# Inverting the heads' triangular matrices on 32x32 diagonal blocks, all four at once, with two slots for the modulation tiles

## What is computed

```python
decay = jnp.exp(jnp.where(lower, g[..., :, None] - g[..., None, :], -jnp.inf))
L = jnp.where(strict, jnp.einsum('bhncd,bhnsd->bhncs', kb, k) * decay, 0.0)
T = lax.linalg.triangular_solve(eye + L, jnp.broadcast_to(eye, L.shape),
                                left_side=True, lower=True, unit_diagonal=True)
u = T @ vb
w = T @ (kb * jnp.exp(g)[..., None])
# then, chunk by chunk: v_new = u - w S;  o = q_dec S + attn v_new;  S = S * g_last + k_dec^T v_new
```

## Time and profile before

| | |
|---|---|
| three executions | 1651.15, 1651.70, 1654.02 us |
| the profiled execution | 1650.68 us, its span 1649.0 us |
| mean granted TensorE clock in the span | 0.997 |
| busy: PE, DVE, ACT, POOL | 97%, 68%, 58%, 30% |
| the rounds, from the first L2410 to the first L2515 | 198.4 to 361.3 us of the span |
| one round | 20.7 us |

### The profile page before, as it was taken

How to read it: one execution, slowest core, us unless ns; L and a number is a source line. 1 busy time by engine, 2 the same in 40 slices (tenths; PEclk the granted TensorE clock), 3 DMA queues, 4 the chain that set the end, 5 groups by cost and what they waited for, 6 DMA issues and landing times.

```text
span 1649.0 us, 33605 instructions
## 1 busy us (share of the span) xinstructions
PE 1594.5 (97%) x11469; PEld 1482.8 (90%) x11477; DVE 1126.0 (68%) x2361; ACT 949.8 (58%) x1811; POOL 491.9 (30%) x406
## 2 busy tenths in 40 slices
PE   7999999999999999999999999999999999999998
PEld 6899899999898899889999999899999888888886
DVE  3787767755556574586469889889898555555554
ACT  1765566664465554563444444689898555544454
POOL 3000256647000005000037777766666100000000
PEclk9999999999999999999999999999999999999999
DMA  9668211138353245247535555554444556666553
GB/s 292 219 185 279 78 52 52 53 121 257 108 154 103 93 158 179 77 128 184 123 112 169 170 173 166 161 152 141 137 138 132 178 191 192 193 193 196 192 191 128
DMA packets 211818, 255.67 MB, mean 155 GB/s; under 512 B 15911, under 2 KB 193803, under 8 KB 211723
## 3 DMA queue, kind: packets, MB, share of 16 engines
q1 hardware_dynamic: 211723, 254.39, 50.5%
HBM read 253.29 MB, written 1.05 MB: 154 GB/s over the span
## 4 chain that ended last, share of the span: by engine, by line
PE 65%; issue 19%; POOL 9%; DVE 3%; ACT 2%; DMA 2%; SPq 1%; POOLq 0%; another core or an unknown queue 0%; DVEq 0%; ACTq 0%
PE ps L2825 21%; PE ps L2234 14%; PE ps L2807 9%; POOL w_lo L721 8%; PE ps L2795 3%; PE ps L2426 2%; PE ps L2515 2%; PE ps L2410 2%; PE ps L2254 1%; PE ps L2406 1%; DMA arena<-in_ada_w 1%; PE ps L2592 1%; POOL arena L711 0%; PE ps L2612 0%; PE ps L2329 0%
## 5 line engine op out<-in xcount | busy, mean ns | idle before, releaser
L721 POOL TENSOR_TENSOR w_lo<-raw,w_hi 128x1024 fp32r<-128x1024 f32 x128 | 307.6, 2407 | 331.7 <-ACT w_hi L1247 331.4
L2234 PE MATMUL ps<-x_hi,w_hi 128*128 128x256 f32 x1088 | 315.2, 290 | 8.1 <-DVE w_lo L1378 3.0
L2234 PE MATMUL ps<-x_lo,w_hi 128*128 128x256 f32 x1088 | 308.3, 283 | 0.0
L2234 PE MATMUL ps<-x_hi,w_lo 128*128 128x256 f32 x1088 | 308.2, 283 | 0.0
L2193 DVE TENSOR_TENSOR w_lo<-raw,w_hi 128x1024 fp32r<-128x1024 f32 x124 | 152.0, 1225 | 143.3 <-ACT w_hi L1356 143.3
L1356 ACT ACTIVATE w_hi<-raw 128x1024 fp32r<-128x1024 f32 x124 | 131.6, 1061 | 167.9 <-PE ps L2825 167.9
L2234 PEld LDWEIGHTS ps<-x_hi,w_hi 128*128 128x128 f32 x1088 | 209.0, 192 | 14.5 <-issue 5.8
L2234 PEld LDWEIGHTS ps<-x_lo,w_hi 128*128 128x128 f32 x1088 | 209.2, 192 | 1.3 <-issue 1.2
L2234 PEld LDWEIGHTS ps<-x_hi,w_lo 128*128 128x128 f32 x1088 | 209.0, 192 | 0.0
L1247 ACT ACTIVATE w_hi<-raw 128x1024 fp32r<-128x1024 f32 x128 | 134.9, 1054 | 110.3 <-DVE raw L1995 110.2
L2770 PE MATMUL ps<-x_hi,w_hi 128*128 128x256 f32 x576 | 165.1, 287 | 9.5 <-ACT arena L1269 8.2
(11 more groups left out here) (432 smaller groups left out, 3734.9 us busy)
## 6 DMA issues: line engine op xcount, KB each, us to landing
raw<-in_u_experts SPq DMA_DIRECT2D x512, 128.0 KB, 2.6
raw<-in_v_experts SPq DMA_DIRECT2D x128, 512.0 KB, 4.3
arena<-in_ada_w SPq DMA_DIRECT2D x22, 1024.0 KB, 7.8
raw<-in_a_w_in SPq DMA_DIRECT2D x12, 1024.0 KB, 5.8
arena<-in_a_w_in SPq DMA_DIRECT2D x12, 1024.0 KB, 5.5
raw<-in_b_w_in SPq DMA_DIRECT2D x8, 1024.0 KB, 5.5
arena<-in_b_w_in SPq DMA_DIRECT2D x8, 1024.0 KB, 5.5
raw<-in_w_in SPq DMA_DIRECT2D x8, 1024.0 KB, 5.4
```

The lines of the kernel that those rows point to most:

```text
L721: pool.tensor_tensor(UTL[e], UT[e % 2], UTH[e].bitcast(F32), ALU.subtract).then_inc(utl_ready, 1)
L2234: ins = mm(o[:, b * S:b * S + S], w[:, slot, kk, b * P:b * P + P], xx[:, (kk + turn) % KC, :], start=(kk == 0 and n == 0), stop=(kk == k - ...
```

## The change

Levels 0 to 3, up to blocks of 32, now touch only the sixteen 32x32 diagonal blocks of the four matrices, packed in one 128x128 tile XC (block q of matrix m in partitions q to q+31 and columns 32m to 32m+31). Each product is 32 deep and 32 wide; the second of a level has 16 moving columns. The transposed copy XC_T is made by DVE (`v.transpose`, within 32x32 blocks) in place of PE's transposition and ACT's copy. Level 4 works on 32x32, level 5 on 64x64 blocks; their results go straight to INVT, the transposed inverse that `finish` reads, and ACT spreads the diagonal blocks into it (`spread`). g no longer alternates.

```diff
+            def diagonal_blocks():
+                return [(m, q, m // 2, 128 * (m % 2) + q) for m in range(4) for q in (0, 32, 64, 96)]
+            def setup_low(r):
+                pe.wait_ge(h_lt, r.nth(1))
+                for m, q, g, at_ in diagonal_blocks():
+                    ins = mm(LOWC[q:q + 32, 32 * m:32 * m + 32], LT[r.side][g][q:q + 32, at_:at_ + 32], ident[q:q + 32, q:q + 32],
+                             start=True, stop=True)
+                ins.then_inc(h_xT, 1)
             def level_p(r, j):
...
-                        for cc in range(2):
-                            ins = pe.transpose(B_[g][:, 256 + cc * 128:384 + cc * 128], xx[:, cc * 128:cc * 128 + 128], ident)
...
+                if j < 4:
+                    for m, q, g, at_ in diagonal_blocks():
+                        ins = mm(PA[q:q + 32, 32 * m:32 * m + 32], lt[g][q:q + 32, at_:at_ + 32], XC[q:q + 32, m, :],
+                                 start=True, stop=True)
+                elif j == 4:
+                    for m, q, g, at_ in diagonal_blocks():
+                        if q % 64 == 0:
+                            ins = mm(PA[q + 32:q + 64, 32 * m:32 * m + 32], lt[g][q:q + 32, at_ + 32:at_ + 64], XC[q:q + 32, m, :],
+                                     start=True, stop=True)
...
+                ins.then_inc(h_p, 1)
             def level_d(r, j):
...
+                if j < 4:
+                    for m, q, g, at_ in diagonal_blocks():
+                        ins = mm(PBC[q:q + 32, 16 * m:16 * m + 16], XC_T[q:q + 32, m, :], PC[q:q + 32, 16 * m:16 * m + 16],
+                                 start=True, stop=True)
...
             def starts(r):
...
+                v.tensor_tensor(XC, LOWC.rearrange("p (m n) -> p m n", m=4), bcast(nm1, 4), ALU.mult).then_inc(h_xt, 1)
+                v.wait_ge(h_xt, r.count(3, 1))
+                v.tensor_tensor(XC, XC, bcast(id32, 4), ALU.add).then_inc(h_xt, 1)
+                v.wait_ge(h_xt, r.count(3, 2))
+                v.transpose(XC_T, XC).then_inc(h_xt, 1)
             def close_level(r, j):
...
+                if j < 4:
+                    xx = left(XC, j)
+                    v.tensor_tensor(xx, xx, dense(PBC, j), ALU.subtract).then_inc(h_xx, 1)
+                    v.wait_ge(h_xx, r.count(12, 2 * j + 1))
+                    v.transpose(XC_T, XC).then_inc(h_xx, 1)
...
-            v.memset(zeroed[:, 0:512], 0.0)
+            v.memset(XPAIR[0:32, :, 32:64], 0.0)
+            v.memset(INVT[0], 0.0)
```

All four blocks q of a product are written to one bank of PSUM (PA is in ps2, PB and PBC in ps3), in four different quarters of the partitions. `turned_over`, `setup_x0`, `starts_low` and the zeroed tiles are gone. The modulation tiles take the slots 2 and 0 by turns, and with XX, LT and BV of the second side moved elsewhere tile 3 of a_w_out is loaded ahead of the rounds:

```diff
-            for u in range(2):
+            for u in (0, 1, 3):
                 load(T_AOUT, 0, u, a_w_out[0, 0:D, :], TW * u)
-            with sp.Fori(0, GQ) as i:
-                sp.wait_ge(raw_free, i + (8 + N_ADA))
...
+            for i in range(GQ):
+                if i == 1:
+                    sp.wait_ge(lo_ready, tile_no(T_AOUT, 0, 0))
+                elif i:
+                    sp.wait_ge(raw_free, 8 + N_ADA + i - 1)
+                slot = MOD_SLOT[i % 2]
```

343 lines of the change are left out of this document (171 added, 172 removed).

## The result

| | before | after |
|---|---|---|
| median of the executions | 1652.1 us | 1637.0 us |
| lowest to highest | 1651.2 to 1654.0 (4) | 1635.0 to 1639.5 (4) |
| the profiled execution, and its span | 1650.7, 1649.0 | 1636.1, 1634.3 |
| mean granted clock in the span | 0.997 | 0.977 |

The change is faster: ratio 0.9908, with a 95% interval of 0.989 to 0.9925, so 15.1 us by the medians. The forecast was 1615 us, 36.7 us less than the 1651.7 of the three executions that it started from. The direction was right, the time lies in the range, and less than half of the gain came.

A forecast was written before the change was run, and what follows sets the result against it. PE's instruction streaming was taken to bound the rounds, 20.7 us each. Eight rounds -29.6, ahead of them -2.8, behind them -3.9: -36.3 us on 1650.7 gives 1614.4, stated as 1615 us; range 1595 to 1664.

The forecast's parts named there:

- The price of p: Time of one 32x32 pass in the inversion: half overlapped, 16 ns, with 328 passes in a round.
- the round's sum: Setup and finish 7.4, level 5 0.9, size changes 2.7, waits 0.5 and 0.3: 11.8 us plus 328 small passes, 17.0 us.
- The other terms of a round: All of a round on PE but its 328 small passes: 11.8 us.
- 0.5 bare and 0.3 behind `lowers`: PE's uncovered waits for DVE in a round: 0.5 us behind level 0's first product, about 0.3 at level 3's close.
- The 19 changes of size: PE switching between full-size work and small products in each round: 0.14 us each, 2.7 us.
- The clock: Rival: the clock falls in the rounds; judged unlikely, chance 0.07 together with a wait not seen.
- 1.2 GHz throughout: The clock rival's priced case: a round about 30 us, the whole 1725 us; chance 0.07 shared with an unseen wait.
- Ahead of round 0: DVE's path to the first mask gets shorter, mask at about 197.9 for 200.72: -2.8 us.
- Behind the rounds: Tile 3 of a_w_out loaded ahead: PE's wait of 2.3 us and the clock fall's 1.6 go, -3.9 us.
- tile 2 is asked for a round earlier: Reason given behind the rounds why tile 2 of a_w_out would not be the next one late; no cost.
- The two slots: Second slot for modulation tiles brings nothing: one slot's chain of 16.1 us is just under a round's 17.0.
- No other engine bounds the rounds: DVE about 12 us a round, ACT under 12, POOL 13.1, all below 17 and hidden by PE's chain: costed at nothing.

## Why the prediction was right and wrong

**The price of p: wrong, on the good side.** 7.7 ns and not 16. The forecast let only the second pass of a block overlap with the first of the next, since "each fp32 product is two passes through the same quarter, one behind the other". The starts show more: a quarter does take a pass only each 28 to 32 ns, as forecast, but all four quarters take theirs within it, 31 / 4 = 7.7. How the two passes of a block come to lie so far apart without holding up the next block was not shown. With 7.7 the round's sum is 11.8 + 328 x 0.0077 = 14.3 us. (The forecast's "60 products" are 48; with the 24 transpositions they make the 120 passes that its sum uses.)

**The other terms of a round: some 1.5 us too low.** At full clock a round takes 15.8 to 15.9; that is read from the versions with dummies, since the change has no round at full clock. Of the missing 1.5, the waits for VectorE explain a part: the four rows above come to 9.7 us, and smaller ones bring it to 11, 1.4 a round, where the forecast had 0.8 (0.5 bare and 0.3 behind `lowers`). The largest is that in front of level 5, for the close of level 4, which the forecast took as covered. The 19 changes of size add 0.4 at 0.32 us a pair for 0.28, by the one place read above. The other 0.5 is open.

**The clock: the step that failed.** "The one fall seen here followed a wait of 2.3 us, and none of the new ones is so long, so it is unlikely", with a chance within 0.07, and so the clock stands in the sum at nothing. The waits are indeed short, 1.1 us at most, and the clock falls all the same, for nearly half of the rounds. The price is in the windows: 16.8 us at a clock of 0.90 (3.4 us at 1.2 GHz), 18.8 at 0.73 (10.2 us): 2.0 us more for 6.8 us, 0.3 for each. The rounds have 144.5 x 0.23 / 0.5 = 66 us at 1.2 GHz, so by this estimate **20 us** are lost; without them the rounds would take 125 us, 38 less than before, and the forecast was 29.6 less. What failed is the inference from one event to a rule on waits: the fall with small dummies came behind 11.5 us of work without a wait. The forecast had the means to doubt it: 164 of the round's products use a sixteenth of the array, and in the stretch of levels 4, 5 and 0 almost nothing of full size stands beside them.

**The place of it in the rivals.** The clock was a rival, but priced only at its extreme (1.2 GHz throughout, 1725 us). A partial fall was the likely form, and its price lies between. Errors of opposite sign brought the rounds to -16.8 us against -29.6: p gave 8.3 ns x 328 x 8 = 22 us more than was forecast, the clock took 20, and the other terms of a round took 12. (These estimates add up to -20; the other 3 us are not accounted for.) That the direction was right was luck in part: by the same estimates, with p at 16 ns and the clock as it was, the rounds would have gained nothing.

**Ahead of round 0: right.** -2.1 by the first mask for -2.8.

**Behind the rounds: wrong.** The wait and the fall at tile 3 went (the clock is 1.00 from 360.4 us on, and the 48 products of a tile take some 6 us where those of tile 3 took 7.5), 3.9 us as forecast. But "tile 2 is asked for a round earlier" looked at its transfer and not at VectorE's order: it is loaded, and its low part stands behind norms and modulation, 1.8 us. The first output products run at 1.2 GHz, and the first nine take 0.9 us more than before (1.92 for 1.07). Together with what is smaller, the place of the tile gains next to nothing, and two runs show it. The expert loop's 3.7 us stand in no row of the kernel before; the forecast had no term for them.

**The two slots: right.** Nothing gained, as said. **No other engine bounds the rounds: right**, DVE is busy 100 us of 144.5, POOL 99.

## What to carry to other kernels

Work that is cut into small pieces of the array may run many times faster, and then lower TensorE's clock for the full-size work around it: price the clock wherever a change takes full-size streaming out of a stretch, even if PE stays busy. Dummy full-size products placed in waits that exist anyway can pay, but only where they are hidden; and dummies in one round can move a fall to another, so look at the clock round by round. A long run of small products can also outrun its own instructions: count them, not only their time. When a wait goes, ask not only for the next transfer but for what stands ahead of it in the order of each engine on its way.

## What the runs showed of the hardware that was not expected

- 32x32 passes in four different quarters of the array start 7.7 ns apart on average, in one quarter 28 to 32 ns, though all of the four quarters' results go to one PSUM bank, each to its own quarter of the partitions. 16 moving columns in place of 32 change nothing in that.
- With full-size bf16 products in four gaps of a round the rounds' clock rose from 0.77 to 0.89; with 32x32 products in the same gaps it was 0.75, and it fell there behind 11.5 us of work without a wait.
- TensorE's instructions arrive, in a long run of small products, at 128 MATMULs with their weight loads per 3.5 to 4.0 us, one 16 KB packet for each piece; the first 218 of the run were there already.
- With 1800 more MATMULs early in TensorE's program a loop 800 us later took 225.7 us for 223.5, and with 1024 more than the change 230.6 for 227.2. The way from one to the other is open.
